# The low part of the seventh weight block of an FFN's Strassen groups, moved from VectorE to GpSimd

## Chip, cores and metric

The kernel runs on one core of one Trainium2 chip (trn2). The metric is the device time in microseconds of one execution. Three runs of the kernel before gave 2321.13, 2326.29 and 2327.1 us, median 2326.29.

## What is computed

The reference is one inference step of a two-layer decoder trunk, for 512 prompt tokens and 64 sample tokens (8 sequences of 8), 576 in all, at a model width of 1024, in float32:

```python
def ffn_half(h, g_pre, g_post, w_in, w_out):
    a = rmsnorm(h, g_pre) @ w_in                      # 1024 -> 2 * 2816
    gate, up = jnp.split(a, 2, axis=-1)
    return h + FFN_RESID * rmsnorm((jax.nn.silu(gate) * up) @ w_out, g_post)
...
for i in range(DEPTH):                                # DEPTH = 2
    yp = ffn_half(yp, g[0], g[1], ffn_w_in[i, 0], ffn_w_out[i, 0])
    # token mixer: layer 0 latent attention (MLA), layer 1 gated linear attention (GLA)
    yp = yp + rmsnorm(mp, g[3])
    yp = ffn_half(yp, g[4], g[5], ffn_w_in[i, 1], ffn_w_out[i, 1])
```

The sample tokens go through the same steps with the same weights. So there are four FFN stages and two mixer stages in the order FFN, MLA, FFN, FFN, GLA, FFN. The change lies in the FFN stages.

## The kernel before

**Number format.** Every float32 operand of a product is held as two float32r tiles, a high part (a copy in the rounded type, made by ScalarE) and a low part (the value minus the high part, made by VectorE or GpSimd). One product of two such operands is three matmuls: high by high, high by low, low by high.

**An FFN stage.** The 2816 gate and up columns are 22 tiles of 128. The first 4 tiles (`CLASSIC`) are plain products. The other 18 (`GRP`) are handled as 18 groups, one tile each. In a group the weights of gate and up form a 2 x 2 block matrix: the two rows are gate and up, the two columns are the halves of the 1024 input features. Each block, `a11`, `a12`, `a21`, `a22`, is a tile of 128 x 512. The tokens are split into two halves of 288. The 2 x 2 by 2 x 2 product is done with seven products in the manner of Strassen and Winograd instead of eight, with four sums of weight blocks `s1` to `s4` and four sums of the tokens `t_1` to `t_4`. The result of the groups, silu(gate) times up, is split into high and low part into the tile `gu`, and an output phase (`out_phase`) multiplies it by the output weights, in blocks of 128 x 1024.

**Order on TensorE** (`group`, line 2415, and `first`, line 2406). For a group g: `s1` by `t_1`, `s2` by `t_2`, `s4`, `s3`, `a12`, then already the first product (`a11`) of group g + 1, and last `a22` by `t_4`, called the seventh product here. Each is 12 matmuls of 288 columns, all recorded under line 2403, 84 matmuls per group. The seventh product takes the high part `a_22_hi`, and the low part `a_22(st, g, 1)`, and waits for the low part (`f_lo`), for `c_3` (`f_c`), and in group 0 for the tokens' low part. After group 17 the output products (line 2341 on) wait for the low part of the first output block (`s_lo`).

**Order on the other engines.** Every engine runs a list in program order; engines meet by semaphores.

- SyncE issues the loads of the four blocks (line 674), `a21` and `a22` of group g + 1 when VectorE has made the sums of group g.
- ScalarE (`group`, line 962) makes the high parts and copies products out of PSUM: line 915 high parts, line 938 PSUM copies `c_1`, `c_2`, `c_3`, line 942 the silu, line 946 the high part of the result, line 954 the high part of `a22` (`hi_a22`), right behind the copy of `c_2` and signalled by `f_22hi`. In the last group `hi_a22` comes later, followed at once by the split of the first output block (line 796).
- VectorE (`group`, line 1702) makes the sums (line 1632), low parts of the sums (line 1659) and of `a11`, `a12` (line 1668), adds products (lines 1681, 1724), scales (1686), multiplies (1699, 1736), and makes the low part of the result (1568, 1570). In group 0 it also makes two low parts of the tokens (line 1615). The low part of `a22` (`low_a22`, line 1674) is made behind line 1724 in group 0 and behind line 1736 in the other groups. It is written in place over `a22`, which `sum_1` must have read before.
- GpSimd (line 1303 on) makes low parts of whole weight blocks (line 1308). In an FFN stage it has nothing to do in the 18 groups: its `ffn` (line 1314) waits for the low part of the eighth block, then takes the output blocks.

Of the kernel before, what the change touches and what calls it, by code (L numbers as in the profile page):

```python
# [7 lines left out]
F32 = mybir.dt.float32  # L8
F32R = mybir.dt.float32r
ALU = mybir.AluOpType  # L10
# [11 lines left out]
GRP = FT - CLASSIC  # L22
# [50 lines left out]
def hybrid_step(nc, io, stages=STAGES):  # L73
    pre_gain = PRE_GAIN
    with ExitStack() as ctx:
        def sem(name):
            return ctx.enter_context(nc.semaphore(name))
# [190 lines left out]
        f_hi, f_sum, f_lo, f_alo, f_p = sem("f_hi"), sem("f_sum"), sem("f_lo"), sem("f_alo"), sem("f_p")  # L268
        f_e, f_c, f_gu = (sem(x) for x in ("f_e", "f_c", "f_gu"))
        f_x, f_thi, f_22hi, f_keep, f_back = (sem(x) for x in ("f_x", "f_thi", "f_22hi", "f_keep", "f_back"))  # L270
# [47 lines left out]
        ffn_no = [sum(k == "ffn" for k in stages[:i]) for i in range(n_st)]  # L318
# [11 lines left out]
        def ring(st, g, i):  # L330

            return bank[(first_unit[st] + 4 * CLASSIC + 3 * (g % 2) + i) % RING]
# [3 lines left out]
        def forms(st):  # L336

            r = first_block[st] % SLOTS
            if r not in made:
                at_of = [[base + 4 * SLOT_W * ((r + j) % SLOTS) + 2 * SLOT_W * i for base in (raw_at, hi_at) for i in range(2)]  # L340
                         for j in range(SLOTS)]
                place = {"a21": at_of[0][0], "a22_0": at_of[0][1], "a11": at_of[0][2], "s1": at_of[0][3],
                         "a11_hi": at_of[1][0], "a11_lo": at_of[1][1], "s2": at_of[1][2], "s2_hi": at_of[1][3],
                         "a12": at_of[2][0], "s4": at_of[2][1], "s4_hi": at_of[2][2], "s3": at_of[2][3],
                         "s3_hi": at_of[3][0], "a12_hi": at_of[3][1], "a12_lo": at_of[3][2], "a22_1": at_of[3][3],
                         "s1_hi": h_at + 4 * T_W}
                w = {n: sb(f"{n}_r{r}", [P, HK * P], F32R if n[-2:] in ("hi", "lo") else F32, offset=o) for n, o in place.items()}
                w |= {f"{n}_lo": sb(f"{n}_lo_r{r}", [P, HK * P], F32R, offset=place[n])
                      for n in ("s1", "s2", "s3", "s4", "a22_0", "a22_1")}
                made[r] = w  # L350
            return made[r]

        def a_22(st, g, part=0):

            n = g % 3 // 2
            return a22_x[part] if g % 3 == 1 else forms(st)[f"a22_{n}_lo" if part else f"a22_{n}"]

        def a_22_hi(st, g):

            return a22_x_hi if g < GRP - 1 else forms(st)["s3_hi"]  # L360
# [943 lines left out]
        def _(pool):  # L1304
# [7 lines left out]
                split_lo(n % SLOTS, n + 1, width[n])  # L1312

            def ffn(st):
                pool.wait_ge(s_lo, first_block[st] + FB)
                out_phase(st, 0)

            def out_phase(st, i0):

                for n in range(out_first[st] + i0, min(first_block[st + 1] + 1, first_block[n_st])):  # L1320
                    low(n)
                if st + 1 < n_st:
                    pool.wait_ge(s_lo, first_block[st + 1] + 2)
                    low(first_block[st + 1] + 2)
                    low(first_block[st + 1] + 3)
# [80 lines left out]
        def _(dve):  # L1406
# [170 lines left out]
            def ffn(st):  # L1577
# [3 lines left out]
                w, g0 = forms(st), GRP * f  # L1581
# [86 lines left out]
                    dve.tensor_tensor(w[f"{name}_lo"][:, :], w[name][:, :], w[f"{name}_hi"][:, :].bitcast(F32),  # L1668
                                      ALU.subtract).then_inc(f_alo, 1)

                def low_a22(g):

                    dve.wait_ge(f_22hi, g0 + g + 1)
                    dve.tensor_tensor(a_22(st, g, 1)[:, :], a_22(st, g)[:, :], a_22_hi(st, g)[:, :].bitcast(F32),
                                      ALU.subtract).then_inc(f_lo, 1)

                def plus(c, ps, copied, made_by):

                    dve.wait_ge(f_e, copied)
                    dve.wait_ge(f_p, made_by)  # L1680
                    dve.tensor_tensor(c[:, :], ps[:, 0:HALF], c[:, :], ALU.add).then_inc(f_c, 1)
# [20 lines left out]
                def group(g):  # L1702
                    a, more = g0 + g, g < GRP - 1
                    if g > 0:
                        last_half(g - 1)
                    low_form("s3", g, 4 if g > 0 else 5, 3)
                    if g > 0:
                        low_part(g - 1, c_1[(g - 1) % 2], 2 * a, 0)
                    if g == 0:
                        x_low_form(1, 3)  # L1710
                    if more:
                        sum_1(g + 1)
                    part_low("a12", g, 6, 6)
                    if more:
                        sum_2(g + 1)
                    plus(c_2, ring(st, g, 1), 3 * a + 3, 7 * a + 4)
                    scaled(c_2, 1, 5 * a + 1)
                    if more:
                        part_low("a11", g + 1, 1, 1)
                    if g == 0:  # L1720
                        x_low_form(2, 4)
                    dve.wait_ge(f_e, 3 * a + 2)
                    dve.wait_ge(f_p, 7 * a + 5)
                    dve.scalar_tensor_tensor(out=c_3[:, :], in0=ring(st, g, 0)[:, 0:HALF], scalar=-1.0, in1=c_3[:, :], op0=ALU.mult,
                                             op1=ALU.subtract).then_inc(f_c, 1)
                    if g == 0:
                        low_a22(g)
                        low_form("s1", g + 1, 2, 2)
                    if more:
                        sum_3(g + 1)  # L1730
                        sum_4(g + 1)
                    if g == 0:
                        low_form("s2", g + 1, 3, 4)
                    dve.wait_ge(s_silu, c0 + 2 * a + 1)
                    dve.wait_ge(f_c, 5 * a + 3)
                    dve.tensor_tensor(c_2[:, :], c_2[:, :], c_3[:, :], ALU.mult).then_inc(f_gu, 1)
                    if g > 0:
                        low_a22(g)
                    plus(c_1[g % 2], ring(st, g, 2), 3 * a + 1, 7 * a + 6)
                    scaled(c_1[g % 2], 0, 5 * a + 4)  # L1740
                    if more and g > 0:
                        low_form("s1", g + 1, 2, 2)
                    low_part(g, c_2, 2 * a + 1, 1)
                    if more and g > 0:
                        low_form("s2", g + 1, 3, 4)
                    if more:
                        low_form("s4", g + 1, 5, 4)
# [455 lines left out]
        def _(pe):  # L2203
# [171 lines left out]
            def ffn(st):  # L2375
# [17 lines left out]
                w, g0 = forms(st), GRP * f  # L2393
# [21 lines left out]
                def group(g):  # L2415
                    a = g0 + g
                    b_a, b_c, b_b = (ring(st, g, j) for j in range(3))
                    pe.wait_ge(f_lo, 5 * a + 1)
                    if g < 2:
                        pe.wait_ge(s_evicted, u0 + 4 * CLASSIC - RING + 3 * g + 2)  # L2420
                    else:
                        pe.wait_ge(f_c, 5 * (a - 2) + 1)
                    if g == 0:
                        pe.wait_ge(f_x, N_FX * f + 9)
                    product(b_c, w["s1_hi"], w["s1_lo"], t_1, True)
                    pe.wait_ge(f_lo, 5 * a + 2)
                    pe.wait_ge(f_e, 3 * a + 1)
                    if g == 0:
                        pe.wait_ge(f_x, N_FX * f + 10)
                    product(b_a, w["s2_hi"], w["s2_lo"] if g > 0 else s2_first, t_2, False)  # L2430
                    pe.wait_ge(f_lo, 5 * a + 3)
                    pe.wait_ge(f_e, 3 * a + 2)
                    product(b_c, w["s4_hi"], w["s4_lo"], b_22, False)
                    pe.wait_ge(f_lo, 5 * a + 4)
                    pe.wait_ge(f_e, 3 * a + 3)
                    if g == 0:
                        pe.wait_ge(f_x, N_FX * f + 11)
                    product(b_a, w["s3_hi"], w["s3_lo"], t_3, False)
                    pe.wait_ge(f_alo, 2 * a + 2)
                    if g < 2:  # L2440
                        pe.wait_ge(s_evicted, u0 + 4 * CLASSIC - RING + 3 * g + 3)
                    else:
                        pe.wait_ge(f_c, 5 * (a - 2) + 4)
                    product(b_b, w["a12_hi"], w["a12_lo"], b_21, True)
                    if g < GRP - 1:
                        first(g + 1)
                    pe.wait_ge(f_lo, 5 * a + 5)
                    pe.wait_ge(f_c, 5 * a + 3)
                    if g == 0:
                        pe.wait_ge(f_x, N_FX * f + 12)  # L2450
                    product(b_a, a_22_hi(st, g), a_22(st, g, 1), t_4, False)
# [536 lines left out]
```

## Time and profile before

| | |
|---|---|
| Median of three runs | 2326.29 us |
| Profiled execution, its own time | 2319.67 us |
| Its span, first to last instruction | 2318.0 us |
| TensorE (PE) busy | 2252.0 us, 97% |
| VectorE (DVE) busy | 1359.6 us, 59% |
| ScalarE (ACT) busy | 1010.9 us, 44% |
| GpSimd (POOL) busy | 458.0 us, 20% |
| TensorE clock granted, mean | 0.997 of full |

The span is what the rows are read against; the execution's own time is 1.67 us more. In the profile PE is TensorE's matmuls, PEld its weight loads, DVE VectorE, ACT ScalarE, POOL GpSimd; `L1674` is line 1674 of the kernel. Names have their buffer numbers left out: `a_lo_r`, `a_x_lo` are low parts, `a_hi_r`, `a_x_hi`, `s_hi_r` high parts, `a_r` and `a_x` the blocks, `s_r` the sums, `c` the tiles `c_1` to `c_3`.

### The profile page before, as it was taken

The numbers are of one execution on the slowest core, as the hardware profiler recorded it, in microseconds if no ns is written. First come the engines' busy times: TensorE is split into PE (matmuls) and PEld (weight loads), VectorE is DVE, ScalarE is ACT, GpSimd is POOL, SyncE is SP. The second block draws the span as 40 slices with busy tenths as digits, with TensorE's granted clock in tenths as the row PEclk, the third lists the DMA queues.
The fourth block names the chain that finished last, engine by engine and source line by source line (L and its number), as shares of the span: only waits on it lengthen the run. The fifth ranks groups of instructions, "written<-read, shape, count | busy, mean of one in ns | idle before, by whom it ended". The sixth has DMA issues, their size and how long they took to land.

```text
span 2318.0 us, 38898 instructions
## 1 busy us (share of the span) xinstructions
PE 2252.0 (97%) x14464; PEld 2034.3 (88%) x14464; DVE 1359.6 (59%) x2767; ACT 1010.9 (44%) x2124; POOL 458.0 (20%) x296
## 2 busy tenths in 40 slices
PE   8999999999899999999999999999999999999998
PEld 8999988986556899998889999888999779999887
DVE  5999700587431689980068998005566647999402
ACT  5555412534322655551255555125322445555322
POOL 1000134250312200004310001432344220000232
PEclk9999999999999999999999999999999999999999
DMA  4223422232671323233232223322211323322422
GB/s 129 78 92 98 144 82 82 73 114 80 215 243 64 113 75 101 96 110 118 82 114 84 95 92 120 108 83 85 72 49 56 147 94 113 102 92 96 142 82 87
DMA packets 100297, 237.59 MB, mean 103 GB/s; under 512 B 12268, under 2 KB 29165, under 8 KB 99854
## 3 DMA queue, kind: packets, MB, share of 16 engines
q1 hardware_dynamic: 97038, 224.62, 29.9%
q0 software_dynamic: 3072, 10.49, 1.4%
q8 instruction: 116, 1.90, 0.3%
q14 instruction: 71, 0.58, 0.1%
HBM read 220.17 MB, written 14.89 MB: 101 GB/s over the span
## 4 chain that ended last, share of the span: by engine, by line
PE 85%; DVE 6%; ACT 3%; DMA 2%; issue 2%; POOL 0%; SPq 0%; DVEq 0%; ACTq 0%; POOLq 0%
PE psum L2403 32%; PE psum L2341 7%; PE psum L2343 7%; PE psum L2342 7%; PE psum L2207 6%; PE psum L2209 6%; PE psum L2208 6%; PE psum L2334 2%; PE psum L2335 2%; PE psum L2626 1%; PE psum L2689 1%; PE psum L2771 1%; DMA a_r<-ffn_in 1%; ACT y L810 1%; DVE y L1456 1%
## 5 line engine op out<-in xcount | busy, mean ns | idle before, releaser
L1308 POOL TENSOR_TENSOR w_lo<-raw,w_hi 128x1024 fp32r<-128x1024 f32 (+1 forms) x157 | 373.5, 2385 | 1640.3 <-ACT w_hi L796 1640.3
L796 ACT ACTIVATE w_hi<-raw 128x1024 fp32r<-128x1024 f32 (+1 forms) x179 | 187.3, 1048 | 454.3 <-DMA raw<-ffn_out 345.1
L1456 DVE TENSOR_TENSOR y<-psum,g_post 128x512 f32<-128x512 f32 x48 | 32.5, 689 | 544.6 <-ACT y L810 544.0
L2207 PE MATMUL psum<-x_hi,w_hi 128*128 128x256 f32 (+1 forms) x1008 | 304.3, 302 | 0.2
L2208 PE MATMUL psum<-x_lo,w_hi 128*128 128x256 f32 (+1 forms) x1008 | 299.5, 297 | 0.0
L2209 PE MATMUL psum<-x_hi,w_lo 128*128 128x256 f32 (+1 forms) x1008 | 299.4, 297 | 0.0
L2341 PE MATMUL psum<-w_hi,gu 128*128 128x512 f32 x704 | 275.2, 391 | 3.2 <-issue 2.6
L2342 PE MATMUL psum<-w_hi,gu 128*128 128x512 f32 x704 | 274.0, 389 | 0.0
L2343 PE MATMUL psum<-w_lo,gu 128*128 128x512 f32 x704 | 274.0, 389 | 0.0
L2403 PE MATMUL psum<-t_lo,s_hi_r 128*128 128x288 f32 x880 | 259.1, 294 | 0.0
L915 ACT ACTIVATE s_hi_r<-s_r 128x512 fp32r<-128x512 f32 x288 | 178.7, 629 | 119.3 <-DVE s_r L1632 118.9
L2207 PEld LDWEIGHTS psum<-x_hi,w_hi 128*128 128x128 f32 x1008 | 192.6, 191 | 3.5 <-POOL w_lo L1308 2.2
L2208 PEld LDWEIGHTS psum<-x_lo,w_hi 128*128 128x128 f32 x1008 | 192.7, 191 | 0.2
L2209 PEld LDWEIGHTS psum<-x_hi,w_lo 128*128 128x128 f32 x1008 | 192.5, 191 | 0.0
L1659 DVE TENSOR_TENSOR s_lo_r<-s_r,s_hi_r 128x512 fp32r<-128x512 f32 x284 | 188.2, 682 | 3.6 <-ACT s_hi_r L915 3.2
L2403 PE MATMUL psum<-x_hi,s_hi_r 128*128 128x288 f32 x576 | 171.2, 297 | 8.0 <-ACT c L938 8.0
L2403 PE MATMUL psum<-x_hi,s_lo_r 128*128 128x288 f32 x576 | 170.4, 296 | 0.0
L2403 PE MATMUL psum<-t_hi,s_hi_r 128*128 128x288 f32 x576 | 169.5, 294 | 0.0
L2403 PE MATMUL psum<-x_hi,a_hi_r 128*128 128x288 f32 x576 | 169.5, 294 | 0.0
L2403 PE MATMUL psum<-x_lo,a_hi_r 128*128 128x288 f32 x576 | 169.4, 294 | 0.0
L2403 PE MATMUL psum<-x_hi,a_lo_r 128*128 128x288 f32 x576 | 169.3, 294 | 0.0
L2403 PE MATMUL psum<-t_hi,s_lo_r 128*128 128x288 f32 x560 | 165.4, 295 | 0.0
(342 smaller groups left out, 5213.4 us busy)
## 6 DMA issues: line engine op xcount, KB each, us to landing
a_r<-ffn_in SPq DMA_DIRECT2D x264, 256.0 KB, 2.8
raw<-ffn_out SPq DMA_DIRECT2D x88, 512.0 KB, 3.6
raw<-ffn_in SPq DMA_DIRECT2D x32, 512.0 KB, 3.7
raw<-gla_in SPq DMA_DIRECT2D x25, 512.0 KB, 3.6
cache<-cache POOLq DMA_DIRECT2D x64, 160.0 KB, 3.3
cache<-cache SPq DMA_DIRECT2D x64, 160.0 KB, 3.4
c_k<-cache_kt SPq DMA_DIRECT2D x64, 128.0 KB, 3.0
a_x<-ffn_in SPq DMA_DIRECT2D x24, 256.0 KB, 2.8
```

The source lines that it names most:

```text
L796: act.activation(w_hi[slot][:, 0:w], raw[slot][:, 0:w], ACT.Copy).then_inc(s_hi, 1)
L915: act.activation(dst[:, :], src[:, :], ACT.Copy).then_inc(f_hi, 1)
L1308: pool.tensor_tensor(w_lo[slot][:, 0:w], raw[slot][:, 0:w], w_hi[slot][:, 0:w].bitcast(F32), ALU.subtract).then_inc(s_lo, 1)
L1456: dve.tensor_tensor(dst, y_bank(b, t, half), post_gain(t, half), ALU.mult).then_inc(s_evicted, 1)
L1659: dve.tensor_tensor((dst or w[f"{name}_lo"])[:, :], w[name][:, :], w[f"{name}_hi"][:, :].bitcast(F32), ALU.subtract).then_inc(f_lo, 1)
L2207: pe.matmul(out, wh, xh, start=start, stop=False)
L2208: pe.matmul(out, wh, xl, start=False, stop=False)
L2209: return pe.matmul(out, wl, xh, start=False, stop=stop)
L2341: pe.matmul(dst, w[0], m[0], start=start, stop=False)
L2342: pe.matmul(dst, w[1], m[0], start=False, stop=False)
L2343: return pe.matmul(dst, w[0], m[1], start=False, stop=stop)
L2403: last = pe.matmul(out[:, 0:HALF], y, m[:, k, :], start=fresh and first, stop=end, skip_group_check=not fresh)
```

## The change

The low part of `a22` is made by GpSimd at the head of its `ffn` instead of by VectorE inside `group`: 18 instructions per FFN stage, 72 in all, of 128 x 512. GpSimd waits for `sum_1` of the group (`f_sum`) and for the high part (`f_22hi`), and signals on `f_22hi`, which so counts two per group; VectorE's count `f_lo` falls from five to four per group, and TensorE's waits are renumbered. Nothing else is changed.

```diff
             def ffn(st):
+                for g in range(GRP):
+                    a = GRP * ffn_no[st] + g
+                    pool.wait_ge(f_sum, 4 * a + 1)
+                    pool.wait_ge(f_22hi, 2 * a + 1)
+                    pool.tensor_tensor(a_22(st, g, 1)[:, :], a_22(st, g)[:, :], a_22_hi(st, g)[:, :].bitcast(F32),
+                                       ALU.subtract).then_inc(f_22hi, 1)
                 pool.wait_ge(s_lo, first_block[st] + FB)
                 out_phase(st, 0)
...
-                def low_a22(g):
-
-                    dve.wait_ge(f_22hi, g0 + g + 1)
-                    dve.tensor_tensor(a_22(st, g, 1)[:, :], a_22(st, g)[:, :], a_22_hi(st, g)[:, :].bitcast(F32),
-                                      ALU.subtract).then_inc(f_lo, 1)
...
                     if g == 0:
-                        low_a22(g)
                         low_form("s1", g + 1, 2, 2)
...
                     dve.tensor_tensor(c_2[:, :], c_2[:, :], c_3[:, :], ALU.mult).then_inc(f_gu, 1)
-                    if g > 0:
-                        low_a22(g)
                     plus(c_1[g % 2], ring(st, g, 2), 3 * a + 1, 7 * a + 6)
...
-                    pe.wait_ge(f_lo, 5 * a + 1)
+                    pe.wait_ge(f_lo, 4 * a + 1)
...
-                    pe.wait_ge(f_lo, 5 * a + 5)
+                    pe.wait_ge(f_22hi, 2 * a + 2)
                     pe.wait_ge(f_c, 5 * a + 3)
```

## Rows read from the trace of the kernel before

**Rows 1.** The page's first part: busy us (share of the span) and instructions by engine.

```profile
PE 2252.0 (97%) x14464; PEld 2034.3 (88%) x14464; DVE 1359.6 (59%) x2767; ACT 1010.9 (44%) x2124; POOL 458.0 (20%) x296
```

**Rows 2.** TensorE's waits, whole span: us in total, times, longest us.

```profile
PE psum L2403 <- ACT c L938: 8.0, 6, 1.9
...
PE psum L2403 <- DVE a_lo_r L1674: 2.4, 8, 0.4
```

**Rows 3.** Stretch 100 to 260 us: busy PE, PEld, DVE, ACT, POOL; clock, DMA share.

```profile
100.00:260.00 160.00, 159.29 (x1202) 159.09 (x1201) 147.84 (x300) 93.87 (x203) 0.00 (x0) 1.00 0.28 93
```

**Rows 4.** Timeline of VectorE, one middle group: start us, us, what, [idle before].

```profile
148.03 0.46 DVE L1681 TENSOR_TENSOR c<-psum,c 128x288 f32<-128x288 f32 x1 [0.67 <-PE psum L2403]
148.52 0.46 DVE L1686 TENSOR_TENSOR c<-c,r_pre 128x288 f32<-128x288 f32 x1
...
151.57 0.68 DVE L1674 TENSOR_TENSOR a_lo_r<-a_r,a_x_hi 128x512 fp32r<-128x512 f32 x1
152.18 0.45 DVE L1681 TENSOR_TENSOR c<-psum,c 128x288 f32<-128x288 f32 x1
...
155.28 0.45 DVE L1699 SCALAR_TENSOR_TENSOR c<-psum,c 128x288 f32<-128x288 f32 x1
...
159.17 0.46 DVE L1681 TENSOR_TENSOR c<-psum,c 128x288 f32<-128x288 f32 x1 [0.67 <-PE psum L2403]
```

**Rows 5.** Timeline of ScalarE, the same group.

```profile
147.02 0.62 ACT L954 ACTIVATE a_x_hi<-a_r 128x512 fp32r<-128x512 f32 x1
...
156.63 0.39 ACT L938 ACTIVATE c<-psum 128x288 f32<-128x288 f32 x1
```

**Rows 6.** Timeline of TensorE: the first matmul of the next group's third product.

```profile
157.30 0.29 PE L2403 MATMUL psum<-x_hi,s_hi_r 128*128 128x288 f32 x1
```

**Rows 7.** GpSimd's groups by shape: count | busy us, mean ns | idle before.

```profile
L1308 POOL TENSOR_TENSOR w_lo<-raw,w_hi 128x1024 fp32r<-128x1024 f32 x149 | 358.7, 2414 | 1624.0 <-ACT w_hi L796 1624.0
...
L1363 POOL TENSOR_TENSOR xl<-xl,qk 128x256 f32<-128x256 f32 x16 | 11.8, 735 | 38.0 <-ACT xl L1202 38.0
```

**Rows 8.** Timeline of VectorE beside GpSimd's low part of rows 9, end of group 17.

```profile
274.69 0.46 DVE L1681 TENSOR_TENSOR c<-psum,c 128x288 f32<-128x288 f32 x1
...
275.18 2.33 DVE L1686 TENSOR_TENSOR c<-c,r_pre 128x288 f32<-128x288 f32 x1
```

**Rows 9.** Timeline, end of group 17 of the first stage: all four engines.

```profile
273.10 0.63 ACT L954 ACTIVATE s_hi_r<-a_r 128x512 fp32r<-128x512 f32 x1 [0.16 <-PE psum L2403]
...
273.68 0.46 DVE L1736 TENSOR_TENSOR c<-c,c 128x288 f32<-128x288 f32 x1
274.05 0.68 DVE L1674 TENSOR_TENSOR a_lo_r<-a_r,s_hi_r 128x512 fp32r<-128x512 f32 x1
...
274.83 2.37 POOL L1308 TENSOR_TENSOR w_lo<-raw,w_hi 128x1024 fp32r<-128x1024 f32 x1 [236.74 <-ACT w_hi L796]
...
274.79 0.40 PE L2403 MATMUL psum<-x_lo,s_hi_r 128*128 128x288 f32 x1 [0.21 <-DVE a_lo_r L1674]
...
277.30 0.47 PE L2341 MATMUL psum<-w_hi,gu 128*128 128x512 f32 x1 [0.64 <-issue]
```

**Rows 10.** Timeline in the MLA stage: GpSimd's line 1336 beside VectorE.

```profile
496.08 1.41 DVE L1834 TENSOR_TENSOR kv_lo<-ckv,kv_hi 128x576 fp32r<-128x576 f32 x2
...
496.62 1.47 POOL L1336 TENSOR_TENSOR qpe<-work,qpe 64x256 fp32r<-64x256 f32 x1 [0.94 <-ACT qpe L1098]
```

**Rows 11.** Timeline in group 0 of the second FFN stage: ScalarE, VectorE, TensorE.

```profile
843.23 0.61 ACT L954 ACTIVATE a_x_hi<-a_r 128x512 fp32r<-128x512 f32 x1
...
843.57 1.35 DVE L1615 TENSOR_TENSOR t_lo<-t_f,x_lo 128x1152 fp32r<-128x1152 f32 x1
...
845.81 0.68 DVE L1659 TENSOR_TENSOR s_lo_r<-s_r,s_hi_r 128x512 fp32r<-128x512 f32 x1
...
845.94 0.40 PE L2403 MATMUL psum<-x_lo,a_x_hi 128*128 128x288 f32 x1 [0.39 <-DVE a_lo_r L1674]
...
852.86 0.37 PE L2403 MATMUL psum<-x_hi,s_hi_r 128*128 128x288 f32 x1 [1.85 <-ACT c L938]
```

More of the change, by code:

```diff
@@ L2425, in group @@
                     product(b_c, w["s1_hi"], w["s1_lo"], t_1, True)
-                    pe.wait_ge(f_lo, 5 * a + 2)
+                    pe.wait_ge(f_lo, 4 * a + 2)
                     pe.wait_ge(f_e, 3 * a + 1)
@@ L2430, in group @@
                     product(b_a, w["s2_hi"], w["s2_lo"] if g > 0 else s2_first, t_2, False)
-                    pe.wait_ge(f_lo, 5 * a + 3)
+                    pe.wait_ge(f_lo, 4 * a + 3)
                     pe.wait_ge(f_e, 3 * a + 2)
                     product(b_c, w["s4_hi"], w["s4_lo"], b_22, False)
-                    pe.wait_ge(f_lo, 5 * a + 4)
+                    pe.wait_ge(f_lo, 4 * a + 4)
                     pe.wait_ge(f_e, 3 * a + 3)
```

## The prediction

> **What bounds the kernel now.** I read the page's first part first. TensorE is busy for 97% of the span, VectorE for 59%, GpSimd for 20% [rows 1]. The change touches only the Strassen groups of the four FFN stages, so the question is what TensorE waits for there. The list of its waits names two producers inside the groups: ScalarE's copies of line 938, 8.0 us in 6 waits, and the low part of the seventh block, line 1674, 2.4 us in 8 waits [rows 2]. Eight waits for 72 such instructions: 64 of them are never waited for. Then the stretch 100 to 260 us, in which the groups of the first stage repeat: TensorE is busy 159.3 of 160 us, VectorE 147.8 (92%), GpSimd not at all [rows 3]. VectorE is nearly full there, but TensorE is the bound.
>
> One group in its middle shows the margin. VectorE's sum of line 1681 starts at 148.03 and again at 159.17, so a group takes 11.14 us, and VectorE idled 0.67 us ahead of it, waiting for TensorE: once per group VectorE is ahead. From 148.03 it runs on end, line 1686 at 148.52, the low part at 151.57, until line 1699 at 155.28 [rows 4]. That releases ScalarE's line 946, behind which, after one more high part, the copy of line 938 ends at 157.02 [rows 5]; the third product that needs it starts at 157.30 without idling [rows 6]. So in a middle group VectorE may fall back 0.28 us before TensorE feels it.
>
> **What is removed.** 72 subtractions of 0.68 us on VectorE. Instructions on VectorE overlap a little, so what one frees is the step from 151.57 to the next start at 152.18, 0.61 us [rows 4]. In a middle group this sits in the run that has 0.28 us of margin and is no bound, so taken alone it gives TensorE nothing.
>
> **What is added.** 72 GpSimd instructions of 512 columns. The rows have 2.41 us for 1024 columns and 0.74 for 256 [rows 7], so 2.2 ns a column and 1.29 us at 512, which I take; half of the one and twice the other bound it, 1.21 and 1.47. It starts some 0.10 us after what it waits for, as GpSimd did at 274.83 behind VectorE's end at 274.73 [rows 9]. GpSimd has nothing else to do in the groups, so its two waits hold nothing behind them but the next group's low part and, after group 17, the first low part of the output weights. The first wait, for the group's own first sum, is met a group earlier. No DMA is moved.
>
> **What it costs VectorE.** The trace has both engines side by side at the end of a stage. Line 1686, two SBUF inputs, takes 0.46 us everywhere else, but 2.33 us when issued at 275.18 into a GpSimd subtraction of 274.83 to 277.20. It ends at 277.51, so its own work began 0.15 us before GpSimd's end. Line 1681, which reads PSUM and one SBUF tile, is not lengthened [rows 8, 9]. The opposite holds too: GpSimd's line 1336, 256 columns, for which rows 7 have 0.74 us, took 1.47 when issued at 496.62 into two such VectorE instructions on end, which were through at 497.49; it let both pass and ended 0.60 us after [rows 10]. So of two instructions that read both inputs from SBUF the later waits for the other's end, and a run of them on VectorE keeps GpSimd out. The Trainium skill ("SBUF — State Buffer", Who interferes with whom) has this as a rule: a VectorE instruction with two SBUF inputs and a GpSimd one that reads SBUF share a read interface, and the second fully blocks. By it offloading buys VectorE little, and the trace agrees.
>
> *Middle group (g = 1 to 16).* ScalarE's high part ends at 147.64 [rows 5]. GpSimd starts near 147.74, while VectorE is idle, and is through at 149.03. Line 1681 passes; line 1686, due at 148.52, begins at 148.88: 0.36 us late. At 151.57 the 0.61 us come back, so VectorE is 0.25 us earlier than before from there on, and the margin ahead of the third product grows to 0.53. The things made inside the late stretch are wanted later: the seventh product starts three products of 11.14 / 7 = 1.59 us before 157.30, at 152.5. TensorE: 0. In the groups that follow, VectorE's lead lets the high part be made earlier and shrinks the 0.36. The cover is the margin of 0.28 plus the 0.61 returned: once line 1686 is held more than 0.89 us, TensorE pays the rest 64 times.
>
> *Group 0, four times.* Here VectorE is late already: the seventh product starts at 845.94, 0.39 us after the previous one, because of the low part, and the third of group 1 at 852.86 after 1.85 us, for a ScalarE copy that stands behind VectorE's line 1699 [rows 11]. The high part ends at 843.84, in the middle of line 1615 (1.35 us, two SBUF inputs, from 843.57). GpSimd waits until 844.92; of its 1.29 us some 0.14 are spent by then (line 1336: 0.60 us after the release instead of 0.74), so it ends near 846.07. The seventh product starts at about 846.1, 0.2 later, which the longer wait in group 1 swallows. VectorE's next subtraction, before at 845.81, can start 0.15 us before GpSimd's end, at 845.92: the chain to group 1 is 0.1 us later. Cost 0.1 us; bounds -0.6 (nothing blocks) and +0.6 (GpSimd gets in ahead of line 1615). I take +0.1 for all four: in two of them the high part ends inside line 1615, in two just ahead of its start, with line 1668 still running; rows 10 show VectorE keeping its turn from one such instruction to the next. Sum: +0.4.
>
> *Group 17, four times.* The high part ends at 273.73, VectorE's line 1736 (two SBUF inputs) runs from 273.68 to 274.14. GpSimd is through at 274.14 + 1.15 = 275.29; before, VectorE had the low part at 274.73. So the seventh product starts 0.55 us later than 274.79. What ends last is something else: TensorE idled 0.64 us before the output product at 277.30, which needs GpSimd's first low part of the output weights, done at 277.20 [rows 9]. That one is queued behind the new instruction: it starts at 275.3 instead of 274.83, and perhaps behind line 1686 too, which now waits first (0.46 us less 0.15 of overlap). It ends at 277.67 to 277.82, so TensorE starts 0.47 to 0.62 later. The seventh product's own delay lies within that. I take 0.55; bounds 0.3 (GpSimd gets in before line 1736) and 0.9. Sum: +2.2.
>
> **The sum.** 64 x 0 + 0.4 + 2.2 = +2.6 us. The profiled execution took 2319.67 us, so 2322.3 for its like; the median of the three runs, 2326.29, lies 6.6 above it, and with that as the base I predict 2329. A measurement of this kernel tells about 0.3%, 7 us, from no change (its three runs lie 6 us apart), so this is no measurable change.
>
> **Rivals.**
> - *The offloading pays.* If the two engines ran without blocking, group 0 would gain 0.6 us and group 17 lose 0.5: 4 x (-0.1), 2326. For it: VectorE is 92% busy and group 1 does wait for its chain. Against it: the 2.33 us of line 1686. For a gain beyond 7 us TensorE would have to be waiting in the middle groups, and it idles 0.7 us in 160. Even all of the waits of rows 2 in the groups come to 10.4 us, several of them for DMA. A measured gain would be scatter: 7%.
> - *VectorE becomes the bound (slower).* Place: line 1686 of the 64 middle groups. If GpSimd's start falls onto it (some 0.6 us later than I put it), or its 512 columns take 1.8 us and not 1.29, VectorE is held up to about 1.14 us, 0.25 beyond the cover of 0.89, and falls back in every group: 64 x 0.25 = 16 us, with the ends 2.6 more, 2345. It decides from 0.11 us past the cover, which is 7 us. For it: 92% busy and the blocking seen. Against it: a start 0.10 us behind the releaser, and VectorE's lead, which grows from group to group and lets the high part come earlier. 13%.
> - *Worst order at both ends only.* GpSimd before line 1615 in group 0 (+0.6) and 0.9 in group 17: 4 x 1.5 = +6, 2332. Still within 0.3%, now and then measured as beyond. 15%.
> - *The change doesn't do what it says:* the low part comes from GpSimd, but nobody's time moves, as when blocking and relief cancel in group 0 and GpSimd is no later in group 17: 2326, 12%.
> - My forecast, 2329: 53%.
>
> **The numbers.** Cases between 2326 and 2332 hold most; the scatter of 3 us either way is added, and the range goes part of the way to the slow rival: 2321 to 2337. Faster by over 0.3%: 0.07; slower: 13% for the rival and some for scatter about +6, 0.16; the same 0.77.
>
> **What would show it.** On the page VectorE's busy time: 72 x 0.68 = 49 us less, but line 1686 takes some of it back; GpSimd gains 72 x 1.29 = 93 us and what it waits while issued. Line 1686 is lengthened to 0.8 or less in middle groups, then shrinks. The wait for line 1674 in TensorE's list is now for GpSimd, eight times, near 0.6 us in group 0 and 0.8 in group 17. Output products start 0.5 us later behind group 17. TensorE stays at 159 of 160 us in the middle. It is wrong if the period of a middle group is above 11.14 us, if line 1686 is held over 0.9, or if the waits for line 938 number dozens rather than six.

## The result and the profile after

The changed kernel takes 2331.12 us (median of 6 runs, 2328.86 to 2334.46), the kernel before 2320.99 (median of 6 runs; three more had come to the three shown above). The ratio is 1.0037, with a 95% interval of 1.0021 to 1.0054: 8.6 us slower by the ratio (the two medians are 10.1 us apart). The result lies in the forecast range, 2321 to 2337, and near the forecast time, 2329. But the likeliest case, no measurable change, did not come about: the kernel is slower by more than three times the 2.6 us of the sum. That it is slower is clear of the noise; whether by more than the 0.3% that was set as the limit is not, since the interval begins at 0.21%. One run of e1 below, 2488.17 us at a mean granted clock of 0.847 against 0.993 to 0.999 in all others, is left out of every comparison.

Below stand the page's first part of the changed kernel, then GpSimd's new instruction in the view by line (count, ns min/median/max) and TensorE's waits. The change moves line numbers: line 2400 is the group matmuls (2403 before), 2338 the first output matmul (2341), 1319 GpSimd's new line, 1735 the multiply (1736), 1574 and 1576 the low part of the result (1568, 1570), 1621 the low part of the tokens (1615), 1638 the sums (1632).

```profile
PE 2255.9 (97%) x14464; PEld 2034.7 (87%) x14464; DVE 1331.2 (57%) x2695; ACT 1016.9 (44%) x2124; POOL 554.3 (24%) x368
```

```profile
L1319 POOL TENSOR_TENSOR a_lo_r<-a_r,a_x_hi x44: 1280/1300/2319, 83.5 to 2153.0; 128x512 fp32r<-128x512 f32 x44
L1319 POOL TENSOR_TENSOR a_x_lo<-a_x,a_x_hi x24: 1287/1298/1301, 94.0 to 2164.2; 128x512 fp32r<-128x512 f32 x24
L1319 POOL TENSOR_TENSOR a_lo_r<-a_r,s_hi_r x4: 1391/1391/1392, 276.0 to 2178.2; 128x512 fp32r<-128x512 f32 x4
```

```profile
PE psum L2400 <- ACT c L938: 8.0, 9, 1.6
...
PE psum L2400 <- POOL a_lo_r L1319: 4.1, 6, 0.7
...
PE psum L2338 <- DVE c L1699: 3.3, 4, 0.8
PE psum L2338 <- issue: 3.2, 4, 0.8
...
PE psum L2400 <- DVE c L1724: 1.9, 2, 0.9
```

VectorE is busy 28 us less, not 49: for the rest it stands longer held by GpSimd, which counts as busy. GpSimd's instruction takes 1.30 us (1.29 was taken). The wait for ScalarE's copies is 8.0 us as in [rows 2]; the wait for the seventh block's low part, 2.4 us there, is now 4.1 for GpSimd and 1.9 for VectorE's line 1724, which was late in two of the four groups 0. And the output products have a wait that the kernel before does not have at all: 3.3 us, four times 0.8, for VectorE's line 1699.

**The middle groups** are as forecast. First the stretch 100 to 260 us, columns as in [rows 3], then VectorE in one group:

```profile
100.00:260.00 160.00, 159.27 (x1200) 158.86 (x1199) 141.76 (x287) 93.90 (x200) 18.18 (x14) 1.00 0.29 95
```

```profile
159.83 0.69 DVE L1638 TENSOR_TENSOR s_r<-s_r,a_r 128x512 f32<-128x512 f32 x1 [0.30 <-PE psum L2400]
161.40 0.46 DVE L1681 TENSOR_TENSOR c<-psum,c 128x288 f32<-128x288 f32 x1 [0.88 <-PE psum L2400]
161.89 0.58 DVE L1686 TENSOR_TENSOR c<-c,r_pre 128x288 f32<-128x288 f32 x1
```

TensorE is as busy as before. Line 1686 is held 0.12 us (0.58 instead of 0.46), not the 0.36 that the forecast began with; in group 1 of the first stage, where VectorE has no lead yet, it takes 0.89, a hold of 0.43. VectorE now idles 0.88 us ahead of line 1681, not 0.67.

**The end of group 17**, four engines in turn (the rows that answer to [rows 9]):

```profile
275.19 0.63 ACT L954 ACTIVATE s_hi_r<-a_r 128x512 fp32r<-128x512 f32 x1 [0.16 <-PE psum L2400]
275.73 1.04 ACT L796 ACTIVATE w_hi<-raw 128x1024 fp32r<-128x1024 f32 x1
...
278.11 1.05 ACT L796 ACTIVATE w_hi<-raw 128x1024 fp32r<-128x1024 f32 x1
```

```profile
275.76 0.46 DVE L1735 TENSOR_TENSOR c<-c,c 128x288 f32<-128x288 f32 x1
...
277.27 0.46 DVE L1686 TENSOR_TENSOR c<-c,r_pre 128x288 f32<-128x288 f32 x1
277.64 2.58 DVE L1574 TENSOR_TENSOR gu<-c,gu 128x224 fp32r<-128x224 f32 x1
280.14 2.40 DVE L1576 TENSOR_TENSOR gu<-c,gu 128x64 fp32r<-128x64 f32 x1
282.47 0.44 DVE L1699 SCALAR_TENSOR_TENSOR c<-psum,c 128x288 f32<-128x288 f32 x1
```

```profile
275.96 1.39 POOL L1319 TENSOR_TENSOR a_lo_r<-a_r,s_hi_r 128x512 fp32r<-128x512 f32 x1 [12.74 <-ACT s_hi_r L954]
277.31 5.15 POOL L1308 TENSOR_TENSOR w_lo<-raw,w_hi 128x1024 fp32r<-128x1024 f32 x2
```

```profile
277.41 0.41 PE L2400 MATMUL psum<-x_lo,s_hi_r 128*128 128x288 f32 x1 [0.74 <-POOL a_lo_r L1319]
280.07 0.47 PE L2338 MATMUL psum<-w_hi,gu 128*128 128x512 f32 x1 [0.79 <-issue]
282.97 0.50 PE L2338 MATMUL psum<-w_hi,gu 128*128 128x512 f32 x1 [0.81 <-DVE c L1699]
```

The low part is ready at 277.35 and the seventh product waits 0.74 us for it, not 0.21; the output products wait 0.79 for GpSimd's first block, not 0.64. That is the delay of the forecast, 0.68 us together. What follows is new. The low part of the result (lines 1574 and 1576, two SBUF inputs each) is issued at 277.64 and 280.14, and each falls into one of two output blocks that GpSimd now makes on end: 2.58 and 2.40 us for work of 0.38 and 0.21 us. Line 1699 stands behind them in VectorE's list and ends at 282.91. The fourth product of the output phase (token tile 2) needs it: by the code it goes into the PSUM bank that line 1699 reads, and waits for `f_gu`.

Before, the same lines went differently:

```profile
277.44 0.38 DVE L1568 TENSOR_TENSOR gu<-c,gu 128x224 fp32r<-128x224 f32 x1
277.74 0.21 DVE L1570 TENSOR_TENSOR gu<-c,gu 128x64 fp32r<-128x64 f32 x1
278.02 0.46 DVE L1699 SCALAR_TENSOR_TENSOR c<-psum,c 128x288 f32<-128x288 f32 x1
...
277.90 1.05 ACT L796 ACTIVATE w_hi<-raw 128x1024 fp32r<-128x1024 f32 x1
...
279.02 7.32 POOL L1308 TENSOR_TENSOR w_lo<-raw,w_hi 128x1024 fp32r<-128x1024 f32 x3 [1.82 <-ACT w_hi L796]
```

There line 1686 was the one held [rows 8]: it was issued 0.35 us after GpSimd's first output block had started. It held up the silu behind it, and so ScalarE's second split, which ended at 278.95. GpSimd idled 1.82 us, and in that time lines 1568, 1570 and 1699 got through. Now the new instruction stands ahead of that block on GpSimd, until 277.35, and line 1686, issued at 277.27, gets its turn between the two. The silu is not held, the second split starts 2.38 us after the first instead of 4.26, and GpSimd has no idle time left. The early finish of one instruction closed the gap that the others had used.

**Group 0.** TensorE's waits ahead of the seventh product of group 0 and the third of group 1, in the four stages, were before 0.39 + 1.57, 0.39 + 1.85, 0.39 + 1.66, 0.39 + 1.56, and are now 0.56 + 1.56, 0.55 + 1.52, 0.94 + 1.56, 0.95 + 1.57. At the seventh product two of the four paid 0.17 us and two 0.55: in the latter GpSimd got in ahead of the token low part (line 1621, 1.35 us), which then took 2.45. Both orders, from the second and the third FFN stage:

```profile
846.01 1.35 DVE L1621 TENSOR_TENSOR t_lo<-t_f,x_lo 128x1152 fp32r<-128x1152 f32 x1
...
846.18 2.32 POOL L1319 TENSOR_TENSOR a_lo_r<-a_r,a_x_hi 128x512 fp32r<-128x512 f32 x1 [44.87 <-ACT a_x_hi L954]
...
1251.81 2.45 DVE L1621 TENSOR_TENSOR t_lo<-t_f,x_lo 128x1152 fp32r<-128x1152 f32 x1
...
1251.61 1.43 POOL L1319 TENSOR_TENSOR a_lo_r<-a_r,a_x_hi 128x512 fp32r<-128x512 f32 x1 [44.50 <-ACT a_x_hi L954]
...
1254.73 0.37 PE L2400 MATMUL psum<-x_lo,a_x_hi 128*128 128x288 f32 x1 [0.94 <-DVE c L1724]
```

**The account.** Waits of TensorE in the four FFN stages, after less before: groups 0 and 1, (3.00 + 6.21) - (1.56 + 6.64) = +1.0; group 17, (2.96 + 3.17) - (0.84 + 2.61) = +2.7; line 1699, +3.3. Together 7.0 us. Waits behind a late load of `a11` in single middle groups were 1.3 us before and 1.8 after; they differ from trace to trace. The two profiled executions lie further apart, 2331.8 against 2319.67 us. Of what is left, 1.8 us is TensorE's wait for the first input load, 10.3 against 8.5 us; the rest lies mostly in the GLA stage, which the change does not touch. There the granted clock stood at its lower level (0.50 in the view by windows) for 3.4 us before, from 1619.9, and for 10.2 us after, from 1625.5 and 1864.4; that this makes the difference fits, but was not tried.

### The profile page after: what moved, and what is told of

Same layout as the page of the kernel before. It is cut to its first block, busy times and chain, and to the rows that moved or that the text cites. A ratio compares the mean times of both kernels' runs of the same rounds, so it can differ in the third digit from the quotient of the medians.

```text
span 2329.9 us, 38970 instructions
## 1 busy us (share of the span) xinstructions
PE 2255.9 (97%) x14464; PEld 2034.7 (87%) x14464; DVE 1331.2 (57%) x2695; ACT 1016.9 (44%) x2124; POOL 554.3 (24%) x368
## 4 chain that ended last, share of the span: by engine, by line
PE 84%; DVE 6%; DMA 3%; ACT 3%; issue 2%; POOL 1%; SPq 0%; DVEq 0%; ACTq 0%; POOLq 0%
PE psum L2400 31%; PE psum L2338 7%; PE psum L2340 7%; PE psum L2339 7%; PE psum L2204 6%; PE psum L2206 6%; PE psum L2205 6%; DMA a_r<-ffn_in 2%; PE psum L2331 2%; PE psum L2332 2%; PE psum L2623 1%; PE psum L2686 1%; PE psum L2768 1%; ACT y L810 1%; DVE y L1462 1%
## 5 line engine op out<-in xcount | busy, mean ns | idle before, releaser
L1319 POOL TENSOR_TENSOR a_lo_r<-a_r,a_x_hi 128x512 fp32r<-128x512 f32 x44 | 59.1, 1343 | 572.3 <-ACT a_x_hi L954 572.3
```

What stands on the lines that cost most here:

```text
L1319: pool.tensor_tensor(a_22(st, g, 1)[:, :], a_22(st, g)[:, :], a_22_hi(st, g)[:, :].bitcast(F32), ALU.subtract).then_inc(f_22hi, 1)
```

## The experiments

The theory: the loss sits at the two ends of each stage's groups, above all behind group 17, and is made of VectorE and GpSimd holding each other up; the middle groups cost nothing. The rival: the middle groups cost, since 64 of the 72 instructions are there. In the kernels below other than e4 the set `ON_DVE` names the groups whose low part VectorE makes, in its old places:

```diff
+ON_DVE = (17,)
...
             def ffn(st):
                 for g in range(GRP):
+                    if g in ON_DVE:
+                        continue
...
+                def low_a22(g):
+
+                    dve.wait_ge(f_22hi, 2 * (g0 + g) + 1)
+                    dve.tensor_tensor(a_22(st, g, 1)[:, :], a_22(st, g)[:, :], a_22_hi(st, g)[:, :].bitcast(F32),
+                                      ALU.subtract).then_inc(f_22hi, 1)
...
                     if g == 0:
+                        if g in ON_DVE:
+                            low_a22(g)
                         low_form("s1", g + 1, 2, 2)
...
+                    if g > 0 and g in ON_DVE:
+                        low_a22(g)
                     plus(c_1[g % 2], ring(st, g, 2), 3 * a + 1, 7 * a + 6)
```

All ratios are against the kernel before, run in the same round on the same chip: 2321.9 us (29 runs) for the first four, 2319.76 (9 runs) for e5 and e6, 2321.32 (23 runs) for e7 and e8. The changed kernel itself stands at 1.0037.

### e1: group 17 back on VectorE

The diff is the one above.

> Group 17's low part goes back to VectorE, groups 0 to 16 stay on GpSimd. Theory (the loss sits at the end of group 17: the seventh product 0.5 us later, the first output block behind it, and VectorE's line 1699 held behind two output blocks on end): the wait of the output products for line 1699 is gone, that for the low part is 0.2 us again, and about 6 of the 8 us come back, 0.25 us of each start of the groups stay: 2 us above before, ratio 1.001. Rival (the loss is spread over the middle groups, where line 1686 is held): about 7 of the 8 us stay, ratio 1.003.

2324.68 us (11 runs), ratio 1.0008 (0.9997 to 1.0018). TensorE's waits, with output products at line 2351 and group matmuls at 2413:

```profile
PE psum L2413 <- ACT c L939: 8.1, 7, 1.8
PE psum L2351 <- issue: 2.6, 4, 0.7
PE psum L2413 <- POOL a_lo_r L1322: 2.2, 4, 0.6
```

The wait for line 1699 is gone and that for the first output block is back at 2.6 us. The four waits for GpSimd left, 0.56 each, are group 0's. Of 0.37%, 0.29 came back (each figure to about 0.1), as the theory says.

### e2: only the middle groups on GpSimd

```diff
+ON_DVE = (0, 17)
```

> Groups 0 and 17 on VectorE as before, groups 1 to 16 on GpSimd. Theory: TensorE's waits in the FFN stages are those of before, time within 1 us of before, ratio 1.000. Rival (middle groups cost): ratio 1.002 to 1.003, and a group's period above 11.14 us.

2324.46 us (12 runs), ratio 1.0013 (1.0003 to 1.0022), 3.0 us where the theory allows 1. The trace shows no place for it. Its span is 2317.8 us, that of the kernel before is 2318.0, and in the stretch 100 to 260 us TensorE does not idle at all:

```profile
100.00:260.00 160.00, 160.00 (x1209) 160.00 (x1208) 141.66 (x287) 96.17 (x203) 19.28 (x15) 1.00 0.29 95
```

What differs is the granted clock. The runs of every kernel here get longer as their mean granted clock falls, e1 from 2319.16 us at 0.998 to 2328.18 at 0.993. A line through all runs, with one level for each kernel, gives 1.6 us for 0.001. The 29 runs before had a mean of 0.9962 and the 12 of e2 0.9950, so the line puts 1.9 us on the clock. At an equal clock e2 is 0.4 us above before, e1 1.0, e3 8.3 and e4 3.5. Whether GpSimd's work lowers the clock or the draw was unlucky is open: the runs of the changed kernel itself had 0.9962.

### e3: only the ends on GpSimd

```diff
+ON_DVE = tuple(range(1, 17))
```

> The opposite: only groups 0 and 17 on GpSimd, groups 1 to 16 on VectorE. Theory: all of the loss is here, 7 to 9 us above before, ratio 1.0035, with the wait for line 1699 of 0.8 us at each of the four output phases. Rival: ratio 1.001 or less.

2331.92 us (5 runs), ratio 1.0043 (1.0028 to 1.0058). Eight of the 72 instructions make a loss as large as that of all 72. (The ratios of e2 and e3 add up to more than the changed kernel's, 1.0056 against 1.0037: some 0.1% of each is scatter.)

```profile
PE psum L2413 <- ACT c L939: 6.1, 4, 1.6
PE psum L2413 <- POOL a_lo_r L1322: 4.6, 7, 0.7
PE psum L2351 <- DVE c L1708: 3.3, 4, 0.8
PE psum L2351 <- issue: 3.2, 4, 0.8
```

The waits behind group 17 are those of the changed kernel to 0.1 us (line 1708 is 1699 there). The rival, that the middle groups make the loss, falls. What e2's time leaves open for them, some 3 us, does not come back in e7 against e8 below.

### e4: line 1699 ahead of the low part

```diff
                     scaled(c_1[g % 2], 0, 5 * a + 4)
...
+                    if not more:
+                        last_half(g)
                     low_part(g, c_2, 2 * a + 1, 1)
...
-                last_half(GRP - 1)
```

> The changed kernel, but in group 17 VectorE makes the last product of the result (line 1699) before the low part of the other half instead of behind it. Theory: the two instructions that are held behind GpSimd's output blocks no longer stand ahead of line 1699, which reads PSUM and is not held; the four waits of 0.8 us are gone, 3.2 us less than the changed kernel, about 5 above before, ratio 1.002. Rival (line 1699 is late for another reason, such as ScalarE's silu): the waits stay, ratio 1.0037.

2327.79 us (11 runs), ratio 1.0025 (1.0014 to 1.0035): 0.12% less than the changed kernel, where 3.2 us are 0.14%. The two intervals overlap, so the time alone does not prove it; against e3, of the same round and with the same waits behind group 17, e4 is 4.1 us faster. What is shown is shown by the trace:

```profile
277.77 0.46 DVE L1699 SCALAR_TENSOR_TENSOR c<-psum,c 128x288 f32<-128x288 f32 x1 [1.65 <-PE psum L2401]
278.15 0.47 DVE L1574 TENSOR_TENSOR gu<-c,gu 128x224 fp32r<-128x224 f32 x1
278.54 2.42 DVE L1576 TENSOR_TENSOR gu<-c,gu 128x64 fp32r<-128x64 f32 x1
280.89 2.67 DVE L1574 TENSOR_TENSOR gu<-c,gu 128x288 fp32r<-128x288 f32 x1
```

VectorE is held as long as in the changed kernel, two instructions of 2.4 and 2.7 us, but nothing that TensorE needs soon stands behind it, and the wait for line 1699 is no longer in its list. The held time was never the price; the instruction queued behind it was. The wait for GpSimd's low part (0.74) and its first block (0.80) stay.

### e5: group 0's high part made early

In group 0 both engines were in each other's way. Some 11 us earlier VectorE has a stretch of instructions that read PSUM. Here `ON_DVE` is `(17,)`.

```diff
                 hi_sum("s2", g0, 2, 3)
+                hi_a22(0)
                 pair(3)
...
                     if more:
-                        hi_a22(g)
+                        if g > 0:
+                            hi_a22(g)
                         hi_sum("s2", a + 1, 2, 3)
```

> Group 17 on VectorE, groups 0 to 16 on GpSimd, and ScalarE makes group 0's high part 11 us earlier, right behind the high part of the first s2, so that GpSimd's low part of group 0 runs beside VectorE's instructions that read PSUM. Theory: VectorE is not held in group 0 and has 0.6 us less to do ahead of group 1; the wait of 0.4 us for the low part is gone and the wait in group 1 shrinks from 1.6 to about 1.0 us: 0.6 us less per FFN stage, 2.4 us below before, ratio 0.999. Rival (the wait in group 1 is set by the load of a11, not by VectorE): nothing below before, ratio 1.000.

2330.64 us (5 runs), ratio 1.0045 (1.0032 to 1.0059): slower, against both. In the first stage the trace shows the gain (203.4 us for its groups, 204.8 before, of which 0.7 are a late load); in the other three there are waits at the start of the groups that no kernel had:

```profile
838.29 0.37 PE L2415 MATMUL psum<-t_hi,s_hi_r 128*128 128x288 f32 x1 [1.32 <-issue]
841.37 0.37 PE L2415 MATMUL psum<-x_hi,s_hi_r 128*128 128x288 f32 x1 [1.24 <-ACT c L939]
```

```profile
835.48 0.63 ACT L955 ACTIVATE a_x_hi<-a_r 128x512 fp32r<-128x512 f32 x1 [4.54 <-PE psum L2415]
836.01 0.76 ACT L881 ACTIVATE work<-work 128x256 f32<-128x256 f32 x2
```

ScalarE idled 4.54 us in front of the moved instruction, for TensorE. `hi_a22` waits for `f_p`, the count of finished products, at 7 (a - 1) + 8, meant as the last product that read the buffer. At the first group of a later stage that count is 7 a + 1, the first product of the stage itself. In its old place the wait was always met; moved ahead, it held the silu behind it, and with it TensorE. The first stage skips the wait (a is 0). So the expectation failed by a wait that I moved without reading it, not by its mechanism; e7 tells the two apart.

### e6: GpSimd started inside VectorE's dense run

```diff
+ON_DVE = (0, 17)
...
                     pool.wait_ge(f_22hi, 2 * a + 1)
+                    pool.wait_ge(f_c, 5 * a + 1)
```

> Groups 0 and 17 on VectorE; in groups 1 to 16 GpSimd waits also for line 1681's first sum (f_c 5a + 1), so it starts when VectorE enters its dense run instead of when VectorE idles. Theory of the prediction (a cover of 0.89 us): VectorE's next instruction with two SBUF inputs is held about 1.1 us, 0.2 us more than the cover, in each of 64 groups: period 11.35 us, 13 us above before, ratio 1.006. Rival (VectorE has more slack than read, or GpSimd is kept out until VectorE's run ends): ratio 1.000 to 1.001.

2349.92 us (4 runs), ratio 1.0121 (1.0105 to 1.0138): 28 us slower, where the prediction's cover gave 13. In this kernel line 1691 is the sum (1681), 1696 the scaling (1686) and 1678 the low part of `a11` (1668 before).

```profile
149.60 0.46 DVE L1691 TENSOR_TENSOR c<-psum,c 128x288 f32<-128x288 f32 x1 [0.60 <-PE psum L2414]
150.09 0.46 DVE L1696 TENSOR_TENSOR c<-c,r_pre 128x288 f32<-128x288 f32 x1
150.47 1.78 DVE L1678 TENSOR_TENSOR a_lo_r<-a_r,a_hi_r 128x512 fp32r<-128x512 f32 x1
...
161.06 0.46 DVE L1691 TENSOR_TENSOR c<-psum,c 128x288 f32<-128x288 f32 x1 [0.61 <-PE psum L2414]
```

```profile
150.23 1.48 POOL L1323 TENSOR_TENSOR a_lo_r<-a_r,a_x_hi 128x512 fp32r<-128x512 f32 x1 [9.97 <-DVE c L1691]
```

The hold is as expected, 1.78 - 0.68 = 1.10 us. The period is 11.46 us, 0.32 above 11.14, and not 0.21; times 64 that is 20 us. The waits for late loads, in single groups, also grew (17 waits for the copies, 16.5 us, against 6 and 8.0); every load is issued behind a VectorE sum, which would explain it, but the cause was not tried. So the cover was read too large: 1.10 less 0.32 leaves 0.78, not 0.89. I had put TensorE's margin at 0.28 us, from the copy's end at 157.02 to the matmul at 157.30. But wherever in these traces a matmul waits for a copy by ScalarE, it starts 0.14 to 0.15 us after the copy's end (852.71 to 852.86 in [rows 11], whose copy is at 852.32 and 0.39 long). By this the margin was 0.13 us and the cover 0.74. Nor is the third product the only place: over the middle groups of this trace, TensorE loses 0.13 us at the first product of a group, behind VectorE's low part of `s1`, and 0.18 at the third. The profile hides both in the modelled length of the matmuls; they show in the steps between matmul starts, 0.24 us and less instead of 0.13.

### e7 and e8: the early high part without the wrong wait

```diff
-                        act.wait_ge(f_p, 7 * (a - 1) + 8 if g < GRP - 1 else 7 * a + 5)
+                        act.wait_ge(f_p, 7 * a if g == 0 else 7 * (a - 1) + 8 if g < GRP - 1 else 7 * a + 5)
```

on e5's kernel is e7; e8 is the same with `ON_DVE = tuple(range(1, 18))`.

> As e5, but ScalarE's early high part of group 0 no longer waits for the first product of its own stage (the wait, written for the buffer's last user, counted one product too many). In e5 the three later stages had new waits of 1.3 and 1.25 us at the start of the groups that the first stage, which has no such wait, did not have. Theory: all four stages are now like e5's first: 0.8 us shorter than before each, 3 us below before, ratio 0.9987. Rival (the early place on ScalarE costs in itself): the waits of e5 stay, ratio 1.003 to 1.0045.

> Only group 0's low part on GpSimd, with the early high part; groups 1 to 17 on VectorE as before. Theory: the gain is all made in group 0, so the same as e7, ratio 0.9987. Rival (GpSimd's work in the middle groups also costs, by a lower granted clock: e2's runs showed 0.9950 against 0.9962 on the mean): e8 is 1 to 2 us faster than e7 and its clock is that of before.

e7 took 2319.77 us (12 runs), ratio 0.9993 (0.9983 to 1.0003), and e8 2321.09 (12 runs), 0.9997 (0.9987 to 1.0007). Neither can be told from no change by its time. The traces show what was meant in both: the waits at the start of the groups are gone, and of group 0's two waits one remains. In e7:

```profile
68.39 1.64 POOL L1324 TENSOR_TENSOR a_lo_r<-a_r,a_x_hi 128x512 fp32r<-128x512 f32 x1 [31.71 <-ACT a_x_hi L955]
```

```profile
PE psum L2415 <- ACT c L939: 6.4, 4, 1.7
PE psum L2353 <- issue: 2.6, 4, 0.7
```

GpSimd's instruction, held 0.3 us by a VectorE low part, then runs beside lines that read PSUM, 12 us ahead of its need. From the first group matmul to the last a stage takes 202.9 to 203.4 us in e7 and e8, and 203.7 to 204.4 before, where two of the four contain a late load of 0.6 to 0.7. That is 0.4 to 0.8 us a stage, 2 to 3 us in all. e7's median is 1.5 us below that of the kernel before in its round, but its interval reaches past 1, and in the round of e5 the kernel before had the same 2319.76: a gain in time is not shown. The rival of e8, that the middle groups cost something through the clock, is not borne out: e7's mean clock was 0.9958 and e8's 0.9955.

## Why the prediction was right and wrong

- **What bounds the kernel, and what the removal gives.** Right. TensorE stays busy in the middle groups, and taking 64 of the 72 subtractions off VectorE's list moves nothing there (e2's trace).
- **What is added.** Right: 1.30 us, forecast 1.29; 1.39 in group 17 and up to 2.32 in group 0, where it is held. Its start was put 0.10 us behind its releaser, from VectorE's end at 274.73; but the row names ScalarE's split, which ended at 274.68, and the new instruction starts 0.14 us behind ScalarE's high part.
- **Middle groups.** Right in sign and mechanism (hold 0.43 in group 1, forecast 0.36, then 0.12), cost 0. The cover of 0.89 us was wrong: e6 shows 0.78, largely because the 0.15 us from a release to the matmul were counted as margin. The slow rival of 13% was thus nearer than I put it, though no group of the changed kernel came near it. Of its two conditions only the late start led there: an instruction of 1.8 us would by the prediction's own working hold line 1686 0.87 us, which is inside 0.89.
- **Group 0.** Forecast +0.1 each, +0.4 in all; measured +1.0 in the profiled execution. The order was not the same in all four: GpSimd went first in two, where the cost was 0.45 and 0.57 us, near the bound of +0.6 that I had named and not taken. In the other two it was +0.16 and -0.17.
- **Group 17.** Here the sum failed. The first output block is 0.7 us later, forecast 0.55. But the term ended there. The prediction wrote that line 1686 now waits first, and did not follow what that releases: the silu, the second split, GpSimd's second block on end of the first, and two VectorE instructions held ahead of line 1699. This wait, 3.3 us, is nearly half of the 7.0 us that TensorE waits longer, and in e4's trace it alone is gone. The term was 2.2 us and measured 6.0.
- **Chances.** Slower by over 0.3% had 0.16, mostly by a mechanism, VectorE as the bound of the middle groups, that e2 and e3 rule out. The right place, the ends of the groups, stood among the rivals at +6 us and just inside the limit, but its 0.9 us for group 17 was GpSimd before line 1736; the wait for line 1699 stood nowhere. That 2329 lies near 2331 is luck: the base was 5.3 us too high (median 2326.29 in three runs, 2320.99 in six), and the sum about as much too low. From the later base the sum gives 2323.6.

## What to carry to other kernels

Moving an instruction to an idle engine was worth nothing here, since the bound lay elsewhere, and it cost at the edges, where the idle engine was about to get work and each held the other up. When a hold goes away, follow what it had been holding back: the kernel before had a gap on GpSimd only because a held instruction delayed the split that would have filled it. What a hold costs is decided by the instruction queued behind it, so a change of order alone can take a wait away while the hold itself stays (e4).

## What the runs showed of the hardware

- Between two VectorE instructions on end, a waiting GpSimd instruction gets its turn if it was issued early enough. In 16 cases of group 0 (four kernels, four stages) GpSimd's was issued from 0.20 us before to 0.37 after VectorE's line 1621. At 0.20, 0.11 and 0.04 us before, GpSimd went first and line 1621 took 2.45 us; at 0.01 before and in all 12 later ones VectorE went first and GpSimd took 2.1 to 2.5. The same program fell to either side in different stages: GpSimd went first in two stages of the changed kernel, in one of e3 and in none of e1 and e4, so part of the changed kernel's cost in group 0 is chance.
- The same turn-taking works for longer runs: behind group 17 VectorE's line 1686, a GpSimd block, VectorE's line 1574, the next block and line 1576 follow each other in turn. So the prediction's reading of [rows 10], that a run on VectorE keeps GpSimd out, does not hold in general. Rows 10 do not fit the 16 cases either: there GpSimd's instruction was issued at 496.62, 0.14 us before the second of VectorE's two (496.75), and still waited for both. What decides a turn so close is open.
- The runs' scatter of some 10 us follows the mean granted clock, 1.6 us for each 0.001 between 0.993 and 0.999 (the line through the runs of all kernels, at e2).
